# Cross attention's two token tiles interleaved, and four moves where the dense front meets the experts

## The reference: what is computed

```
x = x + o @ W_out
x = x + CrossAttn(RMSNorm(x), RMSNorm(mem))      (4 heads of 128 into 256 memory tokens)
x = x + HierMoE(RMSNorm(x))                       (top-1 group of 4, top-2 of its 8 experts)

cross:  q = rms_norm((h @ wq) per head, qn_g);  probs = softmax(q k^T / sqrt(128));  o = (probs v) @ wo
moe:    g_logits = h @ w_group + b_group;  e_logits = h @ w_expert + b_expert
        y = sum over the 2 chosen experts of weight * (silu(h @ w_gate) * (h @ w_up)) @ w_down
```

## Time and profile before

| | us |
|---|---|
| median of 3 runs | 1584.38 (1581.39 to 1585.43) |
| the profiled execution, whole | 1582.93 |
| its span, first to last instruction | 1581.0 |
| PE busy | 1211.7 (77% of the span) |
| DVE busy | 603.4 (38%) |
| ACT busy | 202.5 (13%) |
| DMA, mean over the span | 304 GB/s, 480 MB |

### The profile page before, as it was taken

One profiled execution on the slowest core, in us unless ns is written; L12 is line 12 of the kernel. 1 busy time (PEld: TensorE's weight loads), 2 busy tenths in 40 slices (PEclk: granted clock), 3 DMA queues, 4 the chain that ended last, 5 costly groups with the idle time before them and its releaser, 6 DMA issues.

```text
span 1581.0 us, 19778 instructions
## 1 busy us (share of the span) xinstructions
PE 1211.7 (77%) x8382; PEld 582.9 (37%) x8382; DVE 603.4 (38%) x1403; ACT 202.5 (13%) x435; POOL 14.0 (1%) x31
## 2 busy tenths in 40 slices
PE   5996999977999978796677577677667667667755
PEld 4783564545544444332222222223222222223211
DVE  3399999994401233332122122222213212212212
ACT  3212010245100142110000000000000000000000
POOL 3000000000000000000000000000000000000000
PEclk9998999986999979899889988888889978988887
DMA  9332443410043645799999999999999999999996
GB/s 306 129 133 87 166 174 139 142 65 20 34 176 143 220 186 202 316 420 421 420 421 422 420 421 421 421 421 421 421 421 420 421 421 421 421 421 421 421 420 251
DMA packets 97496, 480.12 MB, mean 304 GB/s; under 512 B 17478, under 2 KB 23750, under 8 KB 45441
## 3 DMA queue, kind: packets, MB, share of 16 engines
q1 hardware_dynamic: 96384, 477.97, 75.0%
q0 software_dynamic: 864, 0.25, 0.1%
q10 hardware_dynamic: 160, 0.64, 0.1%
HBM read 476.71 MB, written 2.11 MB: 303 GB/s over the span
## 4 chain that ended last, share of the span: by engine, by line
DMA 50%; PE 26%; DVE 19%; ACT 3%; issue 2%; SPq 1%; DVEq 0%; ACTq 0%
DMA ring<-in_moe_w_up_dram 32%; DMA late_ring<-in_moe_w_up_dram 16%; PE bank L827 7%; PE bank L939 6%; PE bank L593 3%; DVE oT L1570 3%; PE bank L863 2%; PE bank L579 2%; DMA ring<-in_moe_w_down_dram 2%; DVE ring L1464 2%; DVE ring L1465 2%; DVE ring L1462 2%; DVE ring L1463 2%; DVE ring L1479 1%; DVE ring L1482 1%
## 5 line engine op out<-in xcount | busy, mean ns | idle before, releaser
L1873 DVE TENSOR_TENSOR tokens_out<-tokens_out,bank 128x512 f32<-128x512 f32 x248 | 153.8, 682 | 451.8 <-PE bank L979 451.8
L939 PE MATMUL bank<-ring,x_gathered 128*32 128x256 f32 x2592 | 250.0, 440 | 86.5 <-DMA ring<-in_moe_w_up_dram 60.4
L939 PE MATMUL bank<-late_ring,x_gathered 128*32 128x256 f32 x1504 | 171.2, 440 | 50.4 <-DMA ring<-in_moe_w_up_dram 30.2
L939 PEld LDWEIGHTS bank<-ring,x_gathered 128*32 128x32 f32 x2592 | 121.7, 124 | 208.8 <-issue 180.9
L579 PE MATMUL bank<-ring,hT 128*128 128x512 f32 (+2 forms) x448 | 170.3, 540 | 4.4 <-ACT hT L1045 3.1
L966 PE MATMUL bank<-ring,hidden 128*32 128x512 f32 x640 | 86.8, 631 | 64.6 <-DMA ring<-in_moe_w_down_dram 45.3
L939 PEld LDWEIGHTS bank<-late_ring,x_gathered 128*32 128x32 f32 x1504 | 80.3, 124 | 118.3 <-issue 103.0
L906 PE MATMUL bank<-x_tok,select 128*32 128x512 f32 x512 | 116.2, 1031 | 3.5 <-DVE select L1902 3.2
L579 PEld LDWEIGHTS bank<-ring,hT 128*128 128x128 f32 x448 | 84.5, 190 | 87.6 <-issue 74.1
L827 PE MATMUL bank<-ring,oT 128*128 128x512 f32 x256 | 110.0, 592 | 0.0
L593 PE MATMUL bank<-hT,ring 128*128 128x256 f32 x384 | 86.5, 387 | 4.6 <-DMA ring<-in_w_in_dram 3.9
(11 more groups left out here) (357 smaller groups left out, 1001.4 us busy)
## 6 DMA issues: line engine op xcount, KB each, us to landing
ring<-in_moe_w_gate_dram SPq DMA_DIRECT2D x82, 1024.0 KB, 26.7
ring<-in_moe_w_up_dram SPq DMA_DIRECT2D x80, 1024.0 KB, 27.6
ring<-in_moe_w_down_dram SPq DMA_DIRECT2D x80, 1024.0 KB, 27.1
late_ring<-in_moe_w_up_dram SPq DMA_DIRECT2D x48, 1024.0 KB, 27.1
late_ring<-in_moe_w_down_dram SPq DMA_DIRECT2D x48, 1024.0 KB, 27.6
late_ring<-in_moe_w_gate_dram SPq DMA_DIRECT2D x46, 1024.0 KB, 26.7
ring<-in_w_in_dram SPq DMA_DIRECT2D x20, 1024.0 KB, 9.8
ring<-in_w_out_dram SPq DMA_DIRECT2D x16, 1024.0 KB, 7.5
```

The source lines that it names most:

```text
L939: mm = pe.matmul(gu_bank[SLOTS * c:SLOTS * c + SLOTS, 0:256], XGT[:, at, k % 4, k // 4, :], pieces[c // 2][:, a:a + 256], start=k == 0, st ...
L1873: ins = v.tensor_tensor(y, x, mix[c][:, :], ALU.add)
```

## The change

It reorders cross attention. The task list becomes: `cT0`, `xq0`, `cT1`, then `xq1`'s product in two halves (`cross_query(0)` and `(1)`, both adding into `xq1`'s bank) with `qxT0` and tile 0's scores between them; then tile 0's values `xp0`, `xo0`, `co00`; `qxT1`; `co10`; tile 1's scores; then the rest of tile 0's output quarters, transposes and router products; and then tile 1 from `xp1` on, in its old order. ACT and DVE follow the same order. Four moves at the front's end: SP waits for `tables` only before the run-time loop; `tab`'s product comes after `gate_up(0, 0)`; DVE's `drain_cols(0, 0)` comes before its counting; and `token_weights(0)` moves from ahead of tile 1's `place_tokens(0)` to behind tile 1's `co2`. ACT's `group_exps(0)` moves behind `hT10`.

```diff
-    for tt in range(TT):
-        t += [f"cT{tt}{q}" for q in range(4)] + [f"xq{tt}"]
-    for tt in range(TT):
-        t += [f"qxT{tt}", f"xl{tt}0", f"xl{tt}1"]
-    for tt in range(TT):
-        t += [f"xp{tt}0", f"xp{tt}1", f"xo{tt}", f"co0{tt}"] + ["pos0"] * tt
-        t += [f"co1{tt}", f"hT{tt}0", f"co2{tt}", f"hT{tt}1", f"hT{tt}2", f"co3{tt}", f"hT{tt}3", f"rl{tt}"]
+    t += [f"cT0{q}" for q in range(4)] + ["xq0"] + [f"cT1{q}" for q in range(4)] + ["qxT0", "xl00", "xl01", "xq1"]
+    t += ["xp00", "xp01", "xo0", "co00", "qxT1", "co10", "xl10", "xl11", "hT00", "co20", "hT01", "hT02", "co30", "hT03",
+          "rl0"]
+    t += ["xp10", "xp11", "xo1", "co01", "pos0", "co11", "hT10", "co21", "hT11", "hT12", "co31", "hT13", "rl1"]
...
-            sp.wait_ge(s["tables"], 1)
             for g in range(MOE_RING, PPE * FIRST):
                 sp.wait_ge(s["pieces_done"], g - MOE_RING + 1)
                 expert(g)
+            sp.wait_ge(s["tables"], 1)
...
+            def cross_query(half):
+
+                b = bank[TASK_NO["xq1"] % 8]
+                for q in (2 * half, 2 * half + 1):
+                    arrived(("xq", q))
+                    for c in range(4):
+                        k = 4 * q + c
+                        mm = pe.matmul(b[:, :], HT[:, k, P:T], piece_view(("xq", q))[:, c, :], start=k == 0,
+                                       stop=k == KD - 1)
+                return mm
...
+            cross_turned(0)
+            token_major("xq0", [("xq", q) for q in range(4)], hT, 0, KD, 512)
+            cross_turned(1)
+            pe.wait_ge(s["psum_drained"], TASK_NO["xq1"] - 7)
+            cross_query(0)
+            query_turned(0)
+            cross_scores(0)
+            mm = cross_query(1)
+            fill("xq1")
+            filled(mm)
+
+            cross_values(0)
+            cross_out(0, 0)
+            query_turned(1)
+            cross_out(0, 1)
+            cross_scores(1)
+            turn_quarter(0, 0)
+            cross_out(0, 2)
+            turn_quarter(0, 1)
+            route_quarter(0, 0)
+            turn_quarter(0, 2)
+            route_quarter(0, 1)
+            cross_out(0, 3)
+            route_quarter(0, 2)
+            turn_quarter(0, 3)
+            route_quarter(0, 3)
+
+            cross_values(1)
+            cross_out(1, 0)
+            b = fill("pos0", cols=32)
+            pe.wait_ge(s["choice"], 1)
+            filled(pe.matmul(b, const("ltri"), chosen[:, 0, :], start=True, stop=True))
+            cross_out(1, 1)
...
+            route_quarter(1, 3)
...
-            pe.wait_ge(s["columns"], 1)
-            filled(pe.matmul(fill("tab", cols=2 * TABLE), const("ones"), RT[:, 360:360 + 2 * TABLE],
-                             start=True, stop=True))
...
+                else:
+                    pe.wait_ge(s["columns"], 1)
+                    filled(pe.matmul(fill("tab", cols=2 * TABLE), const("ones"), RT[:, 360:360 + 2 * TABLE],
+                                     start=True, stop=True))
                 gate_up(j, 1, j % 2, arrived_static, place[2:4])
...
+            drain_query(0)
+            drain_scores(0)
+            cross_exps(0)
+            drain("xq1", QX[:, 1, :])
+            drain_values(0)
+            skip("co00")
+            drain_query(1)
+            skip("co10")
+            drain_scores(1)
+            quarter_square(0, 0)
+            drain_turned(0, 0)
+            cross_exps(1)
+            skip("co20")
+            quarter_square(0, 1)
+            drain_turned(0, 1)
+            quarter_square(0, 2)
+            drain_turned(0, 2)
+            skip("co30")
+            quarter_square(0, 3)
+            drain_turned(0, 3)
+            drain("rl0", RL[:, 0, :], cols=36)
+
+            drain_values(1)
+            skip("co01", "pos0", "co11")
+            quarter_square(1, 0)
+            drain_turned(1, 0)
+            group_exps(0)
+            skip("co21")
+            quarter_square(1, 1)
+            drain_turned(1, 1)
+            quarter_square(1, 2)
+            drain_turned(1, 2)
+            skip("co31")
+            quarter_square(1, 3)
+            drain_turned(1, 3)
+            skip("rl1", "pos1")
...
+            def query_norm(n):
+                wait_task(dve, f"xq{n}")
+                head_norm(QX[:, n, :].rearrange("p (r n) -> p r n", n=P), XN, XA_H, P, "qx_n")
+
+            def cross_maximum(n):
                 wait_task(dve, f"xl{n}1")
                 row_maximum(XL[:, n].rearrange("p h w -> p (h w)"), XA_H, T, 4 * n, "xl_max")
-            for n in range(TT):
+
+            def cross_normalise(n):
                 dve.wait_ge(s["xl_exp"], n + 1)
                 normalise(XL[:, n].rearrange("p h w -> p (h w)"), XA_H, T, 4 * n, "xl_p")
 
+            query_norm(0)
+            cross_maximum(0)
+            cross_normalise(0)
+            query_norm(1)
...
-                    token_weights(0, picked[0][2])
                     place_tokens(0)
                     select(0, 0)
-                for c in range(1, 4):
-                    add_residual(f"co{c}{tt}", tt, c)
+                add_residual(f"co1{tt}", tt, 1)
+                if tt == 0:
+                    cross_maximum(1)
+                add_residual(f"co2{tt}", tt, 2)
+                if tt == 0:
+                    cross_normalise(1)
+                else:
+                    token_weights(0, picked[0][2])
+                add_residual(f"co3{tt}", tt, 3)
...
+            gain = bc(GK[:, 6:6 + KD].rearrange("p (c k) -> p k c", c=COLS).unsqueeze(3), [P, 4, COLS, SLOTS])
+
+            def drain_cols(b, at):
+
+                dve.wait_ge(s["x_cols"], tally(b, 1, 1))
+                v.tensor_tensor(XGT[:, at, :, :, :], cols_bank[:, :].rearrange("p (k c s) -> p k c s", k=4, c=COLS), gain,
+                                ALU.mult).then_inc(s["x_cols_out"], 1)
+
+            drain_cols(0, 0)
             wait_task(dve, "cnt")
```

More of the change, by code:

```diff
@@ L829, in _, with cross_turned @@
                     filled(mm)
-            for tt in range(TT):
+            def cross_turned(tt):
                 pe.wait_ge(s["c_n"], tt + 1)
@@ L845, in _, with cross_values @@
                     filled(mm)
-            for n in range(TT):
+            def cross_values(n):
                 pe.wait_ge(s["xl_p"], n + 1)
@@ L871, in route_quarter @@
[L871 to L899, removed]
+            def cross_out(n, c):
+                arrived(("co", c))
+                b = fill(f"co{c}{n}")
+                for k in range(XA_H):
+                    mm = pe.matmul(b, XOT[:, k, P * n:P * n + P], piece_view(("co", c))[:, k, :],
+                                   start=k == 0, stop=k == XA_H - 1)
+                filled(mm)
@@ new lines, in turn_quarter, with route_quarter @@
+            def turn_quarter(n, c):
+                wait_task(pe, f"co{c}{n}")
+                transposes(f"hT{n}{c}", [X[:, n, 512 * c + P * i:512 * c + P * i + P] for i in range(4)])
+            def route_quarter(n, c):
+                wait_task(pe, f"hT{n}{c}")
+                if c == 0:
+                    pe.wait_ge(s["router_w"], 1)
+                    pe.wait_ge(s["psum_drained"], TASK_NO[f"rl{n}"] - 7)
+                b = bank[TASK_NO[f"rl{n}"] % 8][:, 0:36]
+                for k in range(4 * c, 4 * c + 4):
+                    mm = pe.matmul(b, HT[:, k, P * n:P * n + P], WR[:, k, :], start=k == 0, stop=k == KD - 1)
+                if c == 3:
+                    fill(f"rl{n}")
+                    filled(mm)
@@ L1228, in _, with drain_query, drain_scores, cross_exps @@
             wait_turn(act, "cT00")
[L1229 to L1235, removed]
+            drain_model("cT", 0)
+            wait_task(act, "wo31")
+            mean_square(X[:, 1, :], xn_of[1], 149, "c_sq")
+            drain("xq0", QX[:, 0, :])
+            drain_model("cT", 1)
+            def drain_query(n):
+                wait_turn(act, f"qxT{n}")
                 drain(f"qxT{n}", QXT[:, :, P * n:P * n + P], four(4), scale=col("xa_qn_g"))
+            def drain_scores(n):
+                wait_turn(act, f"xl{n}0")
                 for i in range(2):
                     drain(f"xl{n}{i}", XL[:, n, 2 * i:2 * i + 2, :], four(2), scale=float(P) ** -0.5)
-            for n in range(TT):
+            def cross_exps(n):
                 act.wait_ge(s["xl_max"], n + 1)
                 exps(XL[:, n, :, :].rearrange("p h w -> p (h w)"), 4, T, 4 * n, "xl_exp")
+            def drain_values(n):
+                wait_turn(act, f"xp{n}0")
+                for i in range(2):
+                    drain(f"xp{n}{i}", XPT[:, n, 4 * i:4 * i + 4, :], four(4))
+                drain(f"xo{n}", XOT[:, :, P * n:P * n + P], four(4))
+            def drain_turned(n, c):
+                wait_turn(act, f"hT{n}{c}")
+                drain(f"hT{n}{c}", HT[:, 4 * c:4 * c + 4, P * n:P * n + P], four(4))
+            def quarter_square(n, c):
+                wait_task(act, f"co{c}{n}")
```

(29 more changed lines are left out.)

33 lines of the change are left out of this document (11 added, 22 removed).

## The result

The changed kernel takes 1561.67 us (median, 1559.72 to 1564.58) where the kernel before takes 1582.89 (1579.91 to 1585.43): a ratio of 0.9873, 95% interval 0.9852 to 0.9893, or 21.2 us less. Forecast were 22.0 us less and 1560.9. Measured once more on another chip: 1561.93 against 1583.14, 0.9875 (0.9854 to 0.9896).

A forecast was written before the change was run, and what follows sets the result against it. From about 650 us the DMA stream bounds the kernel, its start held back by PE through `gate_up(0, 0)`. 19.4 + 3.1 - 0.5 = 22.0 us off the profiled 1582.93 gives 1560.9; range 1557 to 1568.

The forecast's parts named there:

- The bound: Expert stream from about 650 us: DMA is full, PE faster, so the end moves as much as piece 19's issue.
- Rival 2: Whole kernel: DMA is the limit throughout, so freeing PE gives nothing; time 1583, chance 3%.
- Rival 3: Experts' static loop: a lasting low clock makes PE slower than an expert's 29.9 us of pieces; time 1589, chance 3%.
- The new order: Cross attention, both tiles: fewer PE waits and less cold time start `co01` 19.4 us earlier.
- The places of the waits: Cross attention: PE waits 0.6 us ahead of `xp0`, some 0.3 for `hT01`'s drain, 0.7 ahead of `xo1`.
- rival 1: Cross attention: interleaving jams on the one ordered drain counter; clock fall 4.7 us, with waits 7.7; time 1568.6, chance 14%.
- the softmax chain: Tile 0, beside the query product's second half: 7.5 us of chain against 7.0 of cover, so PE waits 0.6 us.
- the table load's 1.28: Tile 0's softmax on ACT: 1.28 us of load counted between maximum and exponentials, with no drain behind it.
- 1.3 us under `co31`: `token_weights(0)` on DVE: 1.3 us, covered by `co31` at either place; it would cost 1.3 if not covered.
- The four moves: Front's end: `gate_up(0, 0)` starts 3.1 us earlier; by clock, up to 1.4 more gain or 0.3 less.
- Given back: Stream's start: PE waits for `columns` behind `gate_up(0, 0)`; small holes cost 0.5 us, range 0 to 2.
- a fixed tail: Behind the last piece's landing: the last expert's work and the store take 14.6 us, untouched by the change.

The follow-up runs named there:

- a4: Changed kernel with an added SP wait holding piece 19 until eight pieces are used: 1573.48 us against 1585.22 for the kernel before, ratio 0.9928.
- b1: Kernel before with only `group_exps(0)` moved behind `hT10`'s drain and `token_weights(0)` behind tile 1's `co2`: 1578.49 us against 1583.35, ratio 0.9979.
- a1: Kernel before with the four moves alone, cross attention in its old order: 1580.03 us against 1585.22, ratio 0.9975.
- a3: Changed kernel with only SP's wait for `tables` back ahead of piece 19: 1562.33 us against 1585.22 for the kernel before, ratio 0.9858.
- b4: Changed kernel with `xp1` ahead of `co30` and `xo1` behind it: 1559.79 us against 1583.35 for the kernel before, 0.9860; once more 1557.88, 0.9849.

## Why the prediction was right, and where its steps were off

**The bound held.** DMA is idle when piece 19 goes, its share is full from 625 us on, and the end follows piece 19: `a4` shows that without touching anything else. Rival 2 (the stream doesn't care) falls with it. The rule of the Trainium skill (Perfetto Trace Analysis, "Identifying the Most-Contended Engine") that stood beside it, to optimise the most-contended engine first, isn't put to the test by this change: no engine was given less to do (PE is busy for 1211.7 us before and 1210.1 after), and the gain came out of PE's waits. Rival 3 (PE becomes the bound) falls with the stream, at 420 GB/s from 650 to 675 and from 1500 to 1525.

**The new order, predicted 19.4 at `co01`, measured 17.2 and 19.8.** The places of the waits were right: no wait of tile 0 is over 1 us (0.84, 0.99, 0.69, 0.47, 0.77). Two terms had another size. First, `xp1` and `xo1` were taken at 1.07 and 2.0; in the first execution they took 1.95 and 3.78, 2.6 us more, in the second 1.07 and 2.05. The windows of the first:

```profile
581.00:582.00 1.00, 0.66 (x6) 0.66 (x6) 0.83 (x5) 0.28 (x1) 0.00 (x0) 1.00 0.00 0
582.00:583.00 1.00, 1.00 (x7) 1.00 (x7) 0.86 (x5) 0.20 (x1) 0.00 (x0) 0.59 0.00 0
583.00:584.00 1.00, 1.00 (x7) 0.88 (x5) 0.86 (x5) 0.47 (x1) 0.00 (x0) 0.50 0.00 0
...
589.00:590.00 1.00, 0.56 (x2) 0.32 (x3) 0.00 (x0) 0.39 (x1) 0.00 (x0) 1.00 0.67 82
```

That is the clock's part of rival 1 (it falls once more, 4.7 us), in tile 1 rather than tile 0 and without the jam on the drain counter that the rival gave as its cause. Secondly, the softmax chain under the second half of the product was put at 7.5 us and PE's wait at 0.6. It took 6.4 (from the end of the scores near 547.45 to 552.62 + 1.22 = 553.84) and the wait was nil. ACT's and DVE's timelines:

```profile
548.26 1.28 ACT L1125 ACT_TABLE_LOAD   x1
549.81 0.51 ACT L1125 ACTIVATE ring<-ring,small 128x256 f32<-128x256 f32 x1 [0.26 <-DVE small L1688]
```
```profile
549.60 0.17 DVE L1688 TENSOR_SCALAR small<-small 128x4 f32<-128x4 f32 x1
...
552.62 1.22 DVE L1694 TENSOR_TENSOR ring<-ring,small 128x1024 f32<-128x1024 f32 x1
```

I had put the table load's 1.28 between maximum and exponentials. ACT makes it ahead of the exponential's wait, so it runs beside DVE's maximum, and the exponentials start 0.04 behind the maximum's end. The Trainium skill, ScalarE: Activation LUTs, section "What ACT_TABLE_LOAD costs", would have 1.38 us of drain behind the load. The trace does not agree: the first exponential starts 0.27 behind the load's end, and what it waits for is DVE.

**`token_weights(0)` was not just covered work.** The prediction gave its move no role but 1.3 us under `co31`. It is what makes the move of `group_exps(0)` possible at all (see `b1`). The number stands, since those 1.3 us did lie under other work, but a step of the explanation was missing.

**The four moves, predicted 3.1, and 1.4 more or 0.3 less by the clock.** From `gather(0)` to `gate_up(0, 0)` it is 10.33 us where it was 13.50: 3.2, and 3.2 in `a1` (10.30). That product then took 1.99 at the high clock where it took 3.16: 1.2 more, in the first execution. In the second they came to 2.8, and 0.5 less.

**Given back, predicted 0.5 for holes (0 to 2), and a fixed tail.** From piece 19 to the end it is 935.5 us where it was 934.1: 1.4 more, and 0.3 less in the second execution (933.8). The size is within the bounds but the place was wrong. PE's new wait for the counting is there, 2.15 us, and up to the last landing it costs 0.2 us or nothing (919.7 and 919.4, 919.6 before). What was given back in the first execution lies in the tail, which I had taken as fixed at 14.6 us and which was 15.7. There the last expert's 96 products took 7.07 us, partly at the low clock, and PE ended last; in the second they took 5.39 and the tail was 14.5. `a1`, with the late stream, has 7.07 and 15.7 too (see `a3`), so this is the clock's and not the change's.

**Sum.** First execution: 17.2 + 3.2 + 1.2 - 1.4 = 20.2. Second: 19.8 + 2.8 - 0.5 + 0.3 = 22.4. Medians: 21.2 and 21.2. Forecast: 22.0. Its mechanism was right; most of the spread between the two is the clock's. That the first execution comes within 2 us is in part luck: of the 2.6 us that the low clock cost at `xp1` and `xo1`, 1.2 came back because `gate_up(0, 0)` happened to run at the high clock.

## What to carry to other kernels

When an engine waits on a chain through two others, count the idle places of both tiles together before moving work: hiding one chain gave 1.3 or 4.7 us here and hiding both gave 13.0, and the clock was low behind the wait that was left. In front of a full DMA stream, look for what holds the first piece: the last one landed 919.2 to 919.9 us behind it in twelve executions. Then look at who ended last: the work behind the last piece took 14.4 to 16.5 us with the clock of its products, so a small change in the stream's start can't be read from one execution's end (`a3`). Count from a common instruction ahead of the change when two executions are compared: 519.9 to 523.4 us had passed by then, in kernels with the same order of work up to there.

## What the runs showed of the hardware

TensorE's clock isn't fixed by the program. Two executions of the same changed kernel ran the same instructions, up to `turn_rows(0)` with the same waits to within 0.3 us, at different clocks. In the first the granted clock fell from 1.00 at 581 us to 0.50 (1.2 of 2.4 GHz) and was back at 589; the last waits ahead of the fall were 0.47 and 0.77 us, between short products of 36 columns and transposes. It was low once more from 616 to 619 (0.65, 0.50, 0.50, 0.64). In the second it stayed at 1.00 through the first place, and was low from 611 to 625 instead:

```profile
611.00:612.00 1.00, 1.00 (x9) 0.04 (x1) 0.86 (x5) 0.00 (x0) 0.00 (x0) 0.76 0.97 410
612.00:613.00 1.00, 0.60 (x6) 0.46 (x2) 0.86 (x5) 0.00 (x0) 0.00 (x0) 0.50 1.04 442
...
625.00:626.00 1.00, 1.00 (x14) 0.72 (x18) 0.14 (x1) 0.25 (x1) 0.00 (x0) 0.91 0.78 131
```

A fall costs 1 to 3 us where it lies on the path (`xp1` and `xo1` 2.6, `gate_up(0, 0)` 1.2 to 1.7, `co01` in `b4` 1.7, the last expert's 96 products 1.7), so a forecast from one profile has this much play, whatever its mechanism. What decides when it falls is left open.

One PSUM accumulation group that stayed open while PE wrote other banks cost nothing: 7.13 and 7.03 us for the halves, 14.00 for the whole; from each start to that of the next instruction it is 6.97 and 6.87, together 13.84, which is what the whole took before.
